# Layer 1's attention: the queries' low part in two halves, and four small pieces of VectorE's and ScalarE's work in other key tiles

## The reference

```python
def attn_core(q, k, v, scale):
    s = jnp.einsum('bqhd,bkhd->bhqk', q.astype(F32), k.astype(F32)) * scale
    p = jax.nn.softmax(s, axis=-1)
    return jnp.einsum('bhqk,bkhe->bqhe', p, v.astype(F32)).astype(v.dtype)
```

## Time and profile before

| what | value |
|---|---|
| median of three runs | 3234.47 us |
| profiled execution, span from first to last instruction | 3233.6 us |
| TensorE busy in the span | 94% |
| GpSimd, VectorE, ScalarE busy in the span | 71%, 60%, 34% |
| layer 1's attention, about 1889 to 2447 us | 558 us |
| of it, one head | 34.6 us |

### The profile page before, as it was taken

One profiled execution on the slowest core, in us unless ns is written; L12 is line 12 of the kernel. 1 busy time (PEld: TensorE's weight loads), 2 busy tenths in 40 slices (PEclk: granted clock), 3 DMA queues, 4 the chain that ended last, 5 costly groups with the idle time before them and its releaser, 6 DMA issues. The chain is left out here.

```text
span 3233.6 us, 44078 instructions
## 1 busy us (share of the span) xinstructions
PE 3044.6 (94%) x14302; PEld 2491.6 (77%) x14302; DVE 1947.3 (60%) x2544; ACT 1105.4 (34%) x1897; POOL 2288.7 (71%) x2297
## 2 busy tenths in 40 slices
PE   7998998998989999999898989999998999999999
PEld 6777876787968888888676767777776778888887
DVE  6585665777864454454535557777765765454454
ACT  4322775134620110010333446766772410010110
POOL 4584765663498888888623268888887688888885
PEclk9999998999999999999998979999999999999999
DMA  6367323457621111112203441111114211111112
GB/s 237 110 203 202 75 58 117 174 170 262 217 79 59 45 52 60 52 43 65 102 26 105 149 130 41 48 41 40 48 29 141 68 40 58 45 52 58 51 46 85
DMA packets 134922, 297.72 MB, mean 92 GB/s; under 512 B 36449, under 2 KB 69473, under 8 KB 134689
## 3 DMA queue, kind: packets, MB, share of 16 engines
q1 hardware_dynamic: 121632, 252.89, 24.8%
q10 hardware_dynamic: 13184, 43.52, 4.3%
HBM read 251.68 MB, written 44.63 MB: 92 GB/s over the span
## 5 line engine op out<-in xcount | busy, mean ns | idle before, releaser
L1546 POOL TENSOR_TENSOR a_pl<-a_p,a_ph 128x512 fp32r<-128x512 f32 x320 | 451.1, 1430 | 102.9 <-ACT a_p L1491 98.1
L164 PE MATMUL ps<-a_q,a_k 97*128 97x512 f32 x960 | 273.3, 398 | 1.3 <-POOL a_q L1565 1.3
L1490 ACT ACTIVATE a_ph<-ps 128x512 fp32r<-128x512 f32 x320 | 192.2, 601 | 179.4 <-PE ps L164 178.6
L1392 DVE TENSOR_REDUCE a_top<-ps 128x1 f32<-128x512 f32 x256 | 172.3, 687 | 95.4 <-PE ps L1316 95.4
L164 PE MATMUL ps<-hidden,whi 128*128 128x512 f32 x704 | 218.0, 391 | 7.2 <-POOL wlo L1849 4.3
L164 PE MATMUL ps<-mixed_hi,l_whi 128*128 128x512 f32 (+1 forms) x544 | 207.2, 381 | 10.3 <-issue 2.9
L3032 POOL TENSOR_TENSOR l_wlo<-l_raw,l_whi 128x512 fp32r<-128x512 f32 x154 | 200.4, 1301 | 12.8
L164 PEld LDWEIGHTS ps<-a_q,a_k 97*128 97x128 f32 x960 | 179.8, 191 | 38.2 <-issue 1.5
L164 PE MATMUL ps<-mixed_lo,l_whi 128*128 128x512 f32 (+1 forms) x544 | 206.4, 379 | 0.0
L164 PE MATMUL ps<-mixed_hi,l_wlo 128*128 128x512 f32 (+1 forms) x544 | 206.2, 379 | 0.0
L2485 DVE SCALAR_TENSOR_TENSOR residual<-ps,mod,residual 128x512 f32<-128x512 f32 x176 | 132.1, 750 | 109.8 <-PE ps L164 109.8
(11 more groups left out here) (421 smaller groups left out, 8886.3 us busy)
## 6 DMA issues: line engine op xcount, KB each, us to landing
l_raw<-in_w_ffn SPq DMA_DIRECT2D x132, 512.0 KB, 3.9
raw<-in_w_ffn SPq DMA_DIRECT2D x66, 512.0 KB, 3.6
l_row<-in_mod_t ACTq DMA_DIRECT2D x32, 512.0 KB, 4.5
f_vraw<-in_mod_t ACTq DMA_DIRECT2D x24, 512.0 KB, 4.1
a_k<-scratch_k SPq DMA_DIRECT2D x32, 320.0 KB, 6.8
f_raw<-in_w_in SPq DMA_DIRECT2D x16, 512.0 KB, 5.4
l_raw<-in_w_out SPq DMA_DIRECT2D x16, 512.0 KB, 5.2
l_shared_row<-in_mod_t ACTq DMA_DIRECT2D x16, 512.0 KB, 6.3
```

Source lines behind the costliest of these rows:

```text
L164: last = nc.tensor.matmul(out, a, b, start=at == 0, stop=at == n - 1)
L1392: nc.vector.tensor_reduce(top[:, q:q + 1, c], e.ps[:, bank:bank + BANK], AX.X, ALU.max).then_inc(s["auxr"], 1)
L1490: nc.scalar.activation(ph[:, kk % 2, c], b, ACT.Exp).then_inc(s["exp"], 1)
L1546: nc.gpsimd.tensor_tensor(pl[:, kk % 2, c], p[:, kk % 2, c], ph[:, kk % 2, c].bitcast(F32), ALU.subtract).then_inc(s["pl"], 1)
```

## The change

The queries' low part, one subtraction over 1024 queries in tile 3, becomes two over 512, in tiles 2 and 3; so the semaphore `qklo` counts three per head instead of two, in the waits of SyncE and TensorE and in GpSimd's prologue for head 0. The values' low part goes from tile 7 to 6, the output's low part from tile 8 to 7, and on ScalarE the output's high part from tile 8 to 6.

```diff
 def keys_and_queries(h):
-    sp.wait_ge(s["qklo"], h * 2)
+    sp.wait_ge(s["qklo"], h * 3)
...
     pe.wait_ge(s["auxr"], h * AUX + AUX + 2)
-    pe.wait_ge(s["qklo"], h * 2 + 2)
+    pe.wait_ge(s["qklo"], h * 3 + 3)
...
-    if more and kk == 3:
-        queries_low(h + 1, 1 - par)
+    if more and kk in (2, 3):
+        queries_low(h + 1, 1 - par, kk - 2)
...
-    if more and kk == 7:
+    if more and kk == 6:
         values_low(h + 1, 1 - par)
-    if tiles[1] is not None and kk == 8:
+    if tiles[1] is not None and kk == 7:
         low(h - 1, 1 - par, tiles[1])
...
-def queries_low(g, par):
-    dve.wait_ge(s["qkhi"], g * 2 + 2)
-    dve.wait_ge(s["qkact"], g * 2 + 1)
-    nc.vector.tensor_tensor(qs[0:QK1, par, 1, :], whole_queries(0, LAT), qs[0:QK1, par, 0, :].bitcast(F32),
+def queries_low(g, par, x):
+    if x == 0:
+        dve.wait_ge(s["qkhi"], g * 2 + 2)
+    else:
+        dve.wait_ge(s["qkact"], g * 2 + 1)
+    a, b = x * BANK, (x + 1) * BANK
+    nc.vector.tensor_tensor(qs[0:QK1, par, 1, a:b], whole_queries(a, b), qs[0:QK1, par, 0, a:b].bitcast(F32),
                             ALU.subtract).then_inc(s["qklo"], 1)
...
-    if kk == 8 and tiles[1] is not None:
+    if kk == 6 and tiles[1] is not None:
         high(h - 1, 1 - par, tiles[1])
...
-                      (whole_queries(0, LAT), qs[0:QK1, 0, 0, :], qs[0:QK1, 0, 1, :])):
+                      (whole_queries(0, BANK), qs[0:QK1, 0, 0, 0:BANK], qs[0:QK1, 0, 1, 0:BANK]),
+                      (whole_queries(BANK, LAT), qs[0:QK1, 0, 0, BANK:LAT], qs[0:QK1, 0, 1, BANK:LAT])):
```

## The result

The changed kernel takes 3281.66 us (median of four runs, 3276.75 to 3290.23) against 3233.08 before (four runs, 3230.9 to 3235.47): ratio 1.0145, 95% interval 1.013 to 1.0161. It is slower by 47 us. I had forecast 3242 and a range up to 3249.

A forecast was written before the change was run, and what follows sets the result against it. TensorE was taken to bound the stage, busy 33.97 of a head's 34.59 us. Terms 14 x 1.70 = 23.8, -7.2, -8.7 and +0.1 summed to +8.0 us, giving 3242 us, range 3226 to 3249.

The forecast's parts named there:

- Queries' halves (-7.2): Tiles 2 and 3: halving the queries' low part removes TensorE's late matmuls in tile 4, 0.48 us in 15 heads.
- Output's low part to tile 7 (-8.7): Moved from tile 8, it lets the high parts start 1.34 us earlier; TensorE's tile 0 stall goes in 13 heads.
- the values' edit: Values' low part from tile 7 to 6: 0.69 us of interface time while GpSimd waits for ScalarE; costed at nothing.
- The turns and the two kinds of heads: VectorE and GpSimd take turns at the shared interface; GpSimd surely first in even heads, a dead heat in odd ones.
- K: The time at which the keys' low part ends on VectorE, from which the prediction counts later steps of the head.
- rival A: VectorE's divide goes first in odd heads: seven lose 0.56 us instead of 1.70, 3234.5 us; chance 0.30 with mixtures.
- The costly edit: Output's high part to tile 6 on ScalarE: waits for the divide, delaying tile 7's exponentials; 1.70 us per head, GpSimd first.
- Loss 1.70 in tile 7: TensorE waits in tile 7 for GpSimd's late low parts of the exponentials: 1.70 us per head in 14 heads.
- rival C: Output's low part gets ahead of tile 7's last L1546: 15 us more, 3257; chance 0.11 shared with another rival.

The follow-up runs named there:

- both cures: The changed kernel with the output's high part in tile 7 and a tiny GpSimd instruction before tile 6's second low part of the exponentials; 3226.31 us, ratio 0.9973.

## Why the prediction was wrong

*Queries' halves (-7.2):* right. Tile 4's wait is gone; alone they shorten the stage by 7.8 us, 6.9 without the luckier clock of head 0.

*Output's low part to tile 7 (-8.7):* right in the changed kernel, but I called it a matter of that part alone. It needs the values' low part out of tile 7: without that it is a loss (ratio 1.0018), with it the stage is 10.4 us shorter. I had costed the values' edit at nothing.

*The turns and the two kinds of heads:* right to a few hundredths. The keys' low part ends 17.8 us behind the head's first value product in both kernels, so it moved with tile 0's stall and not with tile 4's. Even heads had GpSimd first, and the divide lasted 2.25; the divide ended at K + 3.47, where my chain has K + 3.48. In odd heads I leaned to GpSimd; five of seven went the other way, as rival A had it, at 34.07 us where I had computed 34.0. The 0.11 us between them held in every head of every kernel, K + 1.22 or 1.23 in even ones and K + 1.12 or 1.13 in odd ones. I had tied it to the partitions that the divide writes, by the rule of the Trainium skill (VectorE: DVE Perf Modes, Two Vector instructions with no wait between them) on outputs in another quadrant; the traces agree.

*The costly edit by itself:* I had 0.56 us per head as its cost with the divide first; alone it made heads 0.4 and 0.54 us longer, 6.5 us of stage.

*Loss 1.70 in tile 7:* the first failing step. "Output's low part comes ready at about 2132.2, behind the start of the last L1546": I had it at K + 7.25 and it came at K + 6.97. GpSimd's turn, at K + 6.95 in my chain, came at K + 7.11, because the output's high part started 0.14 us behind the divide, not 0.06, and the exponentials followed it without the 0.1 of overlap. So the order was the other one. The prediction doesn't show how it came to 2132.2, so which part of that time was 0.28 too long can't be said. It is rival C, to which I gave a small part of 0.11: the waits are 2.79 us, not 1.70. With the output's low part back in tile 8 they are 1.82.

*The clock:* the second and larger failing step, a term that the sum didn't have. I costed a wait of TensorE at its length. Of the nine long heads' +51.3 us, the waits less the gains explain 9 x (2.79 - 1.16) = 14.7; the rest, 36.6 us, agrees with 78.5 us at half clock, which can cost 39. The runs show it apart from the waits: 4.6 us per head, gone when the first wait is filled with useless matmuls. I had seen clock 1.00 in the head of the earlier trace rows and not asked what idle time would end it. The Trainium skill (TensorE: Matmul & The Clock Gate, The HAM clock gate) says that TensorE runs at 1.2 GHz by default and that activity releases the throttle; the traces agree on the two levels, with matmuls following each other by 0.43 and 0.23 us.

With the first error mended the sum by heads, nine of the long kind and five of the short, would have been about +12 us, some 3246, still inside my range; the clock makes it +48. The direction, slower, came out as forecast, but three quarters of the loss came by a term that I didn't have.

## What to carry to other kernels

A stall that is taken away moves every engine that ran behind it, but not those held by something else. The order of two instructions at a shared interface can turn on a tenth of a microsecond, so a piece whose wait hangs on it should not stand ahead of work on the critical chain. Cost an idle time of TensorE not only by its length: here two new waits of 2.8 us together brought on, in most heads, a fall of the clock that cost up to 4.6 us more, while one of 1.4 us alone brought none. A run in which a wait is filled with useless work tells the two costs apart. Try coupled moves one by one and together: here the queries' halves alone were not told from no change, the output's parts alone were a loss, and the output's parts with the values' low part were -0.3%.

## What the runs showed of the hardware that I had not expected

- A GpSimd and a VectorE instruction with two SBUF inputs each, starting within a hundredth of a microsecond of each other (2106.99): VectorE went first in five odd heads of the changed kernel, GpSimd in two, by the same program. Over the six kernels with such ties VectorE went first in 25 of 42. Starting 0.03 or 0.04 earlier it went first in all seven even heads (2119.72 and 2119.76); starting 0.1 later it was second in all 42.
- TensorE's clock at 0.50 for 10.24 or 3.41 us, after two waits that add up to 2.7 or 2.8 us with 0.8 us of matmuls between them: in nine heads of nine in one kernel, in two of three and one of three in others; after 1.38 and 0.44 us in two of eight; after one wait of 1.41 us in none of seven, after 0.4 us in tile 6 and 0.4 in tile 7 in none of seven.
- The stage's gains in the traces arrive in the timed ratios unevenly: of 7.8 us some 3 (the queries' halves alone), of 10.0 some 5 (the high part in tile 7), of 11.4 some 9 (both cures), of 10.4 all 10 (output and values), with intervals of 3 us each way. How long TensorE is at half clock outside of the stage differs from trace to trace (118 to 161 us ahead of the stage, 17 to 31 after it), and why is open.
